# One block for the output projection, the norm and the queries, and a last stage with the activations stationary

## The reference

```
x  = x + gate1 * (merged @ w_out)                      # 1024x1024 by 1024x1024
h2 = rms_norm(x, norm2_w) * (1 + scale2) + shift2      # over the 1024 channels of a token
q  = (h2 @ w_q).reshape(B, S, 8, 2, 128)               # 16 units of 128 columns
s  = einsum('bshpd,hpkd->bshpk', q, keys)              # 128 scores for each token and unit
top_s, top_i = top_k(s, 16)                            # then 16 experts of 16384 for each head
y  = sum over the chosen experts of gate * gelu(h2 . u[e]) * v[e]
x  = x + gate2 * y
```

## Time and profile before

| | |
|---|---|
| median of 3 runs | 3905.96 us |
| the profiled execution | 3907.96 us |
| its span, first to last instruction | 3906.2 us |
| TensorE matmul busy | 3656.0 us (94% of the span) |
| TensorE weight load busy | 3391.5 us (87%) |
| VectorE busy | 2631.3 us (67%) |
| ScalarE busy | 1268.6 us (32%) |
| GpSimd busy | 591.9 us (15%) |
| granted TensorE clock, mean | 0.965 |

### The profile page before, as it was taken

The page is one execution under the profiler, slowest core; times in us unless marked ns, Lnnn a source line. Parts: engine busy times, 40 slices in busy tenths (PEclk is TensorE's granted clock), DMA queues, the critical chain, the costliest instruction groups (busy, mean ns, idle before and its releaser), DMA issues. The chain is left out here.

```text
span 3906.2 us, 60440 instructions
## 1 busy us (share of the span) xinstructions
PE 3656.0 (94%) x21828; PEld 3391.5 (87%) x21828; DVE 2631.3 (67%) x5338; ACT 1268.6 (32%) x1755; POOL 591.9 (15%) x516
## 2 busy tenths in 40 slices
PE   5899999799599697999999999999899999999999
PEld 2677776687487696999999999999899999999999
DVE  5133443488443687587878888788587777888887
ACT  3133343377211311223232232323233333333332
POOL 0000000000000000122222323232122222222221
PEclk8999999899799798999999999999999999999999
DMA  7312110111433112566877868595899999999997
GB/s 284 131 60 64 44 55 28 52 57 38 140 107 109 49 38 94 193 220 219 276 251 245 279 218 300 198 329 167 277 381 347 346 347 347 355 359 346 347 347 269
DMA packets 372789, 811.74 MB, mean 208 GB/s; under 512 B 30720, under 2 KB 207744, under 8 KB 369152
## 3 DMA queue, kind: packets, MB, share of 16 engines
q1 hardware_dynamic: 298880, 540.81, 39.6%
q0 software_dynamic: 73728, 268.47, 19.8%
HBM read 679.66 MB, written 129.50 MB: 207 GB/s over the span
## 5 line engine op out<-in xcount | busy, mean ns | idle before, releaser
L80 PE MATMUL s_ps_a<-back_dense_hi,s_u_hi 128*128 128x384 f32 x2048 | 703.1, 343 | 26.5 <-DVE s_u_lo L1648 26.5
L80 PE MATMUL c_ps_y<-c_wa_hi,c_v_hi 128*128 128x384 f32 x2048 | 688.6, 336 | 22.7 <-DVE c_wa_lo L1984 22.7
L81 PE MATMUL c_ps_y<-c_wa_lo,c_v_hi 128*128 128x384 f32 x2048 | 687.1, 335 | 0.0
L82 PE MATMUL c_ps_y<-c_wa_hi,c_v_lo 128*128 128x384 f32 x2048 | 687.1, 335 | 0.0
L82 PE MATMUL s_ps_a<-back_dense_hi,s_u_lo 128*128 128x384 f32 x2048 | 686.3, 335 | 0.0
L81 PE MATMUL s_ps_a<-back_dense_lo,s_u_hi 128*128 128x384 f32 x2048 | 685.8, 335 | 0.0
L1963 ACT ACTIVATE c_v_hi<-c_v_raw 128x1024 fp32r<-128x1024 f32 x256 | 271.7, 1062 | 669.6 <-PE c_ps_y L82 619.6
L1585 POOL DMA_INDIRECT s_row<-in_u_rows,back_expert x128 | 161.4, 1261 | 2022.8 <-DVE back_expert L1750 1603.0
L1982 DVE TENSOR_TENSOR c_v_lo<-c_v_raw,c_v_hi 128x1024 fp32r<-128x1024 f32 x256 | 313.5, 1225 | 203.7 <-ACT c_v_hi L1963 203.5
L80 PEld LDWEIGHTS s_ps_a<-back_dense_hi,s_u_hi 128*128 128x128 f32 x2048 | 386.0, 188 | 26.7 <-DVE s_u_lo L1648 26.7
L80 PEld LDWEIGHTS c_ps_y<-c_wa_hi,c_v_hi 128*128 128x128 f32 x2048 | 386.9, 189 | 24.4 <-DVE c_v_lo L1982 23.9
(11 more groups left out here) (329 smaller groups left out, 6695.0 us busy)
## 6 DMA issues: line engine op xcount, KB each, us to landing
c_v_raw<-in_v SPq DMA_DIRECT2D x256, 512.0 KB, 6.4
s_u_raw<-in_u SPq DMA_DIRECT2D x128, 512.0 KB, 4.8
act_scratch<-s_a SPq DMA_DIRECT2D x128, 384.0 KB, 4.1
gm_scratch<-s_gm SPq DMA_DIRECT2D x48, 1024.0 KB, 10.5
c_a<-act_scratch SPq DMA_DIRECT2D x256, 192.0 KB, 3.5
c_g<-gm_scratch SPq DMA_DIRECT2D x256, 192.0 KB, 4.4
a_w<-in_w_ada SPq DMA_DIRECT2D x24, 1024.0 KB, 7.8
q_raw<-in_w_pq SPq DMA_DIRECT2D x17, 512.0 KB, 3.6
```

The lines of the kernel that those rows point to most:

```text
L80: nc.tensor.matmul(out, w_hi, x_hi, start=first, stop=False)
L81: nc.tensor.matmul(out, w_hi, x_lo, start=False, stop=False)
L82: return nc.tensor.matmul(out, w_lo, x_hi, start=False, stop=last)
```

## The change

Two independent parts.

First, `project` and `route` become one block `project_and_route` (names `p_` throughout, the weights in `merged_raw`, `merged_w_hi`, `merged_w_lo`), without a barrier between, the loops written out:

```diff
+            for j in range(TT):
+                last = nc.tensor.matmul(ps_ms[:, j:j + 1], total[:, j * P:(j + 1) * P], ones[:], start=True, stop=True)
+            last.then_inc(summed, 1)
...
+            for j in range(TT):
+                last = nc.tensor.transpose(ps_rstd[:, j * P:(j + 1) * P], spread[:, j * P:(j + 1) * P], ident[:])
...
-            for c0, c1 in split_columns(T):
-                last = nc.tensor.matmul(ps_sum[:, c0:c1], ones[:], total[:, c0:c1], start=True, stop=True)
...
-            nc.vector.reciprocal(x[:, 1], x[:, 0]).then_inc(rstd_done, 1)
+            nc.vector.reciprocal(rstd[:], root[:]).then_inc(rstd_done, 1)
+            nc.vector.tensor_copy(spread.rearrange("p (j o) -> p j o", o=P), rstd[:].rearrange("p (j o) -> p j o", o=1).broadcast_to([P, TT, P]))\
...
-            for k in range(KD):
-                nc.vector.tensor_tensor(x1[:, k], x1[:, k], x[:, 1], ALU.mult).then_inc(normed, 1)
+            normalise(0)
+            normalise(1)
             for k in range(KD):
+                if k + 2 < KD:
+                    normalise(k + 2)
                 for n, (hi, lo, tokens) in enumerate(halves(k)):
...
+            for k in range(KD):
+                pe.wait_ge(h2_lo_done, 2 * k + 1)
+                for c0, c1 in ((0, HALF), (HALF, TD)):
+                    last = query(0, k, c0, c1)
...
+            for u in range(1, UNITS):
+                bank(u, 0).then_inc(half_done, 1)
+                scores(u - 1)
+                if u == 1:
+                    token_rows(1)
+                bank(u, 1).then_inc(half_done, 1)
+            scores(UNITS - 1)
```

Second, `combine`: 128 tokens' activations are the stationary operand and `v` streams in 512 columns, 3 token tiles by 2 halves by 3 matmuls = 18 for a chunk. The result has tokens on partitions, so it is copied out of 6 banks (`y_out`), transposed by TensorE into `ps_t` (two banks), and finished as before:

```diff
-                for k in range(KD):
-                    end = product3(nc, ps_y[:, k, 0:W], v_hi[:, s, k * P:(k + 1) * P], v_lo[:, s, k * P:(k + 1) * P], wa_hi[:, s], wa_lo[:, s], first, last)
-                    if last:
-                        nc.tensor.transpose(ps_y[:, k, W:HALF], (keep.y, y)[h][:, k * P:(k + 1) * P], ident[:]).then_inc(y_ready, 1)
+                for i in range(TILES):
+                    for n in range(2):
+                        end = product3(nc, ps_y[:, 2 * i + n], wa_hi[:, s, i * P:(i + 1) * P], wa_lo[:, s, i * P:(i + 1) * P],
+                                       v_hi[:, s, n * HALF:(n + 1) * HALF], v_lo[:, s, n * HALF:(n + 1) * HALF], first, last)
...
+            def turn(h, k):
+                for i in range(TILES):
+                    nc.tensor.transpose(ps_t[:, k % 2, i * P:(i + 1) * P], y_out[:, i, k * P:(k + 1) * P], ident[:])
+                nc.tensor.transpose(ps_t[:, k % 2, W:HALF], (keep.y, y)[h][:, k * P:(k + 1) * P], ident[:]).then_inc(turned, 1)
...
+            for c in range(RING * PEEL):
+                chunk(1, c, c % RING, c == 0, False)
+                if c % 2 == 1 and c < KD:
+                    turn(0, c - 1)
+                    turn(0, c)
...
+            for c in range(RING * (PEEL + 1)):
+                load(1, c, c % RING)
+            results(0)
+            sp.wait_ge(stored, 16 * KD)
+            x1_load(1)
```

More of the change, by code:

```diff
@@ new lines, in query, with bank, token_rows @@
+            def query(u, k, c0, c1):
+                return product3(nc, acc[:, u % 2, c0:c1], w_hi[:, u % 2, k], w_lo[:, u % 2, k], *h2(k, c0, c1), k == 0, k == KD - 1)
+            def bank(u, n):
+                for c0, c1 in TOKEN_BANKS[n]:
+                    for k in range(KD):
+                        last = query(u, k, c0, c1)
+                return last
+            def token_rows(g):
+                for k in range(KD):
+                    out, tile = score[:, 1, k * P:(k + 1) * P], (TD + g * P, TD + (g + 1) * P)
@@ new lines, in _ @@
+            pe.wait_ge(lo_done, KD - LOADED + 1)
+            for k in range(KD):
+                pe.wait_ge(h2_lo_done, 2 * k + 1)
+                for c0, c1 in ((0, HALF), (HALF, TD)):
+                    last = query(0, k, c0, c1)
+                    if k == KD - 1 and c0 == 0:
+                        last.then_inc(half_done, 1)
+            pe.wait_ge(h2_lo_done, 2 * KD)
+            for k in range(KD):
+                last = query(0, k, TD, T)
+            last.then_inc(half_done, 1)
@@ new lines, in evict @@
+            def evict(h):
+                if h >= 1:
+                    act.wait_ge(turned, KD * h)
+                for i in range(TILES):
+                    act.wait_ge(y_ready, BANKS * h + 2 * i + 1)
+                    nc.scalar.activation(y_out[:, i, 0:HALF], ps_y[:, 2 * i], ACT.Copy).then_inc(y_left, 1)
+            act.sem_inc(y_used, RING)
+            with act.Fori(0, NK // RING) as i:
+                for s in range(RING):
+                    chunk(0, i, RING * i + s, s)
+            for s in range(RING):
+                if s == RING - 1:
+                    evict(0)
+                chunk(1, 0, s, s)
@@ L1973, in _ @@
+            nc.vector.memset(y[:], 0.0).then_inc(y_zero, 1)
+            with dve.Fori(0, NK // RING) as i:
+                for s in range(RING):
+                    chunk(0, i, RING * i + s, s)
+                    dot(i, bass.ds(RING * i + s, 1), s)
+            for c in range(RING * PEEL):
+                s = c % RING
+                if c == RING - 1:
+                    evict(0)
+                chunk(1, c // RING, c, s)
+                if c == RING:
                     dve.wait_ge(y_zero, 1)
@@ new lines, in _ @@
+                if c >= RING:
+                    add(c // RING, c, slice(c, c + 1), s)
+                    if c % 2 == 0:
+                        finish(0, c - RING)
+                        finish(0, c - RING + 1)
+            with dve.Fori(PEEL, NK // RING) as i:
+                for s in range(RING):
+                    chunk(1, i, RING * i + s, s)
+                    add(i, RING * i + s, bass.ds(RING * i + s, 1), s)
+            evict(1)
+            for k in range(KD):
+                finish(1, k)
```

512 lines of the change are left out of this document (264 added, 248 removed).

## The result

The changed kernel takes **3879.1 us** (median of 4 runs, 3876.4 to 3880.6) where the kernel before takes 3905.7 (4 runs on the same chip, 3903.5 to 3908.2): a ratio of 0.9931, interval 0.9914 to 0.9948, so 26.6 us less. The forecast was 3872, 33.7 less than 3905.7. The sign came out, and so did the way in which most of the time is won. The two halves split otherwise than forecast. In the profiled executions the block of queries ends 21.6 us earlier, 3.3 more than the term of -18.3, and of that 20.9 us have arrived where the last stage starts. The last stage, from its first matmul to the program's end, is 6.5 us shorter (1079.4 after 1086.0), 9.6 less than the term of -16.1.

What follows compares the result with a forecast made beforehand. TensorE, 94% busy, was taken as the bound. Norm and queries -18.3 and last stage -16.1 (-20.5, -1.3, +5.7) sum to -34.4 us: 3872 us. Its own range was 3862 to 3881, and 3861 to 3889 to hold 8 in 10.

Steps and rivals of the forecast that it cites:

- the term of -18.3: Norm and queries: ScalarE starts 4.3 us earlier, unit 1 25.0 earlier, of which 18.3 us arrive at the block's end.
- the term of -16.1: Last stage together: steady part -20.5, between the passes -1.3, tail +5.7, in all -16.1 us.
- Steady part, -20.5: Last stage: a chunk takes 4.080 us after 4.160, by fewer, wider matmuls; -20.5 us over 256 chunks.
- rival D: Fixed cost per matmul is 2.5 ns, the rest stays in each chunk: -17.7 in all, 3888 us; chance 0.03.
- The rival in which data takes over (A): Last stage's chunk stays at 4.16 us because DMA is really full at 0.95: 3892 us; chance 0.08.
- The tail, +5.7: From the last chunk's start to VectorE's end: 11.8 us after 6.2, so +5.7; bounds +4.7 and +8.
- Between the passes, -1.3: Change of passes in the last stage: 5.1 us lost after 6.4, so -1.3; bounds -3 and +10.
- rival B: Ring runs dry early in second pass; TensorE stands 8 to 12 us, restarts at lower clock: 3884 us; chance 0.10.
- One of the prediction's own signs of being wrong: Last stage: the prediction called itself wrong if SyncE's wait shows up as waits of TensorE.
- the forecast's own range: Whole kernel: 3862 to 3881 us, from bounds -13 and -22, +4.7 and +8, -3 and +4.
- the +10 that the passage names as the bound: Change of passes: upper bound, for SyncE standing behind the results' stores before it issues x1 and chunk 16.

Runs made afterwards that it cites:

- the first and third experiments: Both against the change: first, SyncE's wait for stores and second x1 load moved after chunk 63, 3868.6 us; third, first pass's result stores left out, 3865.9 us.
- the first experiment: Against the change, SyncE waits for the first pass's stores and loads the second x1 only after chunk 63, not before chunk 16: 3868.6 us, ratio 0.9905.

## Why the prediction was right, and where it was wrong

**Steady part, -20.5: right.** 4.079 us a chunk; the fixed 13.3 ns a matmul that I read from three pitches came back at 13.7 in the run with 256 columns. The Trainium skill (TensorE: Matmul & The Clock Gate, Back-to-back issue gap) has 2.5 ns for a matmul by itself, and says that in a stream the weight loads count too, which the prediction and its rival D leave out. For these matmuls of a high and a low part, each with a weight load of its own, no row shows so little, and the measurement decides. The rival in which data takes over (A) fell with the same row: 353 GB/s over 370 us of unbroken TensorE. The Trainium skill's 358 GB/s (DMA: Bandwidth & Descriptors, Specifications) is no ceiling on this core either: 414 GB/s in the run without the third product. The Trainium skill (Perfetto Trace Analysis, Roofline) says that a core alone can go beyond that share, and here the trace agrees.

**The tail, +5.7: right.** From the last chunk's start (last matmul 3868.39 less 17 x 0.2267) to VectorE's end it is 11.8 us, the sum of the terms. (The prediction's "about 7 us" from the last matmul to the last finish is 8.0 by the same rows.)

```profile
3870.46 5.91 DVE L2063 SCALAR_TENSOR_TENSOR c_x<-c_ps_t,keep_mod,c_x 128x512 f32<-128x512 f32 x8 [0.95 <-PE c_ps_t L2127]
```

**Between the passes, -1.3: the step that failed.** At the change of passes itself it came as reckoned: TensorE idle for 0.30 us, VectorE's one wait for a gathered row 2.32. But of SyncE behind the stores I wrote that "the data has 12.5 - 6.4 = 6 us to spare, and the split chunks ahead of TensorE some 9 more, so I price it at nothing". Two numbers in that were wrong. I reckoned 7 to 10 us for eight issues and a landing; it took 16.4, 5.7 for the issues and 10.6 for the landing. The 6.4 us is the median landing of v in the whole run, taken for stores that land among full queues, and for v behind 2 MB of x1, which took 10.6 as well (3396.36 to 3406.92). Counted out from the rows above: TensorE was through with chunk 15 at 3409.85 - 7.35 = 3402.50, 24.5 us after the first store's issue, and into these had to go 16.4 until x1's issue, 12.5 until chunk 16's v was there, and 2.9 for its split, 31.8 us. That is rival B, to which I gave 0.10, at 3884. Of the causes that it lists, SyncE behind the stores is the one that the first and third experiments show; VectorE's late work stood as it was in both, and the gap was gone. It had the size ("8 to 12 us and restart at the lower clock"), and what it cost is the 10.5 us between the change and the first experiment. One of the prediction's own signs of being wrong came true with it: SyncE's wait showed up as a wait of TensorE.

That the time still lies within the stated range is partly luck. The gap took 10.5 us and the first half gave back 3.3 for reasons of its own; without these 3.3 the time would be 3882, above the forecast's own range (3862 to 3881). That range isn't what its bounds give, either: with -22 or -13, -20.5, -3 or +4, +4.7 or +8 it would be 3865 to 3884. And the +10 that the passage names as the bound for just this step (SyncE behind the stores) went into the range as +4, with no reason given, while the step measured -1.3 + 10.5 = +9.2.

**Norm and queries, -18.3: right in kind, 3.3 too small.** Unit 1 started 2.0 us earlier than reckoned: I had charged unit 0 with the lower clock again, but early queries had brought it to full by 1280 (0.98 from 1280 to 1285). VectorE's last two units took 20.9, not 21.4, and the queries between ran 0.8 us faster than 14 units of my pace: 3.3 in all, from 1510.4 down to 1507.1. Its parts were also measured one at a time: the early queries are worth 5.7 us by the medians (9.4 in their place), the short norm 4.3 by the medians (6.5 by rows; forecast 4.3). What remains of the 21.6 is some 12 us if the medians are taken off and some 6 if the rows are. I put it down to the merge of the two blocks (no barrier, first loads and first split between them). That is by difference and shown by no experiment, and its size is open within that span.

The sum, with the terms as measured: -21.6 in the first half; in the second -20.7 + 5.6 - 1.3 + 10.5 = -5.9; together -27.5, against -26.6 by the medians and -27.4 between the spans of the two profiled executions. The term of 10.5 is the difference of two medians.

The best kernel of the study has both loads of x1 late: 3860.8 us, 18 less than the change and 45 less than the kernel before.

## What to carry to other kernels

A queue that issues the loads of a ring must not wait for a landing: put the wait so far behind the issue that it is met when it is reached, and a large load that is needed late behind the small ones that are needed now. Here the late load of 2 MB costs nothing while TensorE is the bound, and makes the next data some 8 us later when DMA is. Price a wait for DMA by the landing at that place, with the queues as full as they will be there, and count the spare time from when the next load would have been issued, not from when it is wanted. Where TensorE is the bound, fewer and wider matmuls are worth the fixed part that the pitch shows, 13 ns each here with its weight load, until the next engine's time per chunk is reached.

## What was not expected of the hardware

- The same 256 KB stores land late in a full stage: SyncE waited 10.6 us behind the last of eight issues in the change, while in the kernel before, where SyncE had issued no load for some 10 us ahead of the stores and VectorE's finishes spaced them out, x1's load followed 1.7 us after the last store's issue. At the end of the program the change waits 1.7 us for its last store as well (2.8 in the run with the left banks first).
- In the run with the wide norm the granted clock was at full from 1280 to 1290, in spite of a wait of some 1 us at each tile. It then fell to 0.66 on the mean from 1290 to 1295, when TensorE had work almost without a break. The change has three waits of 0.8 to 1.0 us at its tiles from 1282 to 1288 and kept 1.00; the wide norm's run has three of 1.0 and then one of 0.8, up to 1290. So a stage of short waits can lose its clock after it had it. The stretches of that run:

```profile
1280.00:1285.00 5.00, 3.23 (x16) 2.32 (x14) 5.00 (x7) 4.88 (x7) 0.00 (x0) 0.99 0.00 0
1285.00:1290.00 5.00, 2.62 (x12) 1.96 (x12) 4.16 (x7) 4.94 (x8) 0.00 (x0) 1.00 0.00 0
1290.00:1295.00 5.00, 4.95 (x23) 4.41 (x24) 1.53 (x3) 0.95 (x3) 0.00 (x0) 0.66 0.00 0
```
